# Small tables change places with a pad: the large buffers of a 28,000-instruction kernel move by 128 or 192 bytes

## The reference

```python
for l in range(DEPTH):                                   # 2 layers
    mix = token_mixer(h, w_in[l], ...)                   # h @ w_in (1024 x 9232), two attention branches,
                                                         # w_pa, w_pb and w_o (each 1024 x 1024)
    h = layer_norm(ALPHA * h + mix, ln1_g[l], ln1_b[l])
    if l % 2 == 0:
        f = swiglu(h, ...)                               # layer 0: dense, hidden width 2816
    else:
        f = moe_swiglu(h, ...)                           # layer 1: 8 experts, 2 chosen per token, hidden 3584
    h = layer_norm(ALPHA * h + f, ln2_g[l], ln2_b[l])
return h[:, N_META:]

def swiglu(x, w_gate, w_up, w_down):
    return (jax.nn.silu(x @ w_gate) * (x @ w_up)) @ w_down
```

## The kernel before

| buffer | before | mod 256 | after | mod 256 |
|---|---|---|---|---|
| raw | 4224 | 128 | 4352 | 0 |
| w_hi, w_lo | 53376, 77952 | 128 | 53504, 78080 | 0 |
| hF, acc | 102528, 111232 | 128 | 102656, 111360 | 0 |
| hT_hi, hT_lo | 115776, 126016 | 64 | 115904, 126144 | 192 |
| tab (the identity first) | 136256 | 64 | 136384 | 192 |
| mT, zT, o_tok, sgA, sgB (row 0) | from 147680 | 224 | from 147488 | 32 |
| aT_hi, aT_lo | 147776, 175936 | 64 | 147584, 175744 | 128 |
| x, S, ST, xg, a_sl, ag, y (experts) | from 147776 | 64 | from 147584 | 128 |

## Time and profile before

### The profile page before, as it was taken

How to read it: one execution, slowest core, us unless ns; L and a number is a source line. 1 busy time by engine, 2 the same in 40 slices (tenths; PEclk the granted TensorE clock), 3 DMA queues, 4 the chain that set the end, 5 groups by cost and what they waited for, 6 DMA issues and landing times.

```text
span 1867.5 us, 28534 instructions
## 1 busy us (share of the span) xinstructions
PE 1831.5 (98%) x11042; PEld 1624.1 (87%) x11042; DVE 1389.9 (74%) x1167; ACT 1101.1 (59%) x857; POOL 37.2 (2%) x78
## 2 busy tenths in 40 slices
PE   8999999999999999999999999999999999999996
PEld 8999999999989999998888888888888888888885
DVE  4756566645556566667888888888898888888987
ACT  5544254543445442546777777777777777777774
POOL 0200100000002001000000000000000000000000
PEclk9999999999999999998999999999999999999999
DMA  8625434444535355254999999999999999899993
GB/s 326 205 97 199 159 114 180 158 159 164 197 126 198 125 199 205 94 201 164 360 371 354 364 341 351 362 369 357 358 333 363 369 357 367 333 354 362 360 370 129
DMA packets 72977, 492.76 MB, mean 264 GB/s; under 512 B 9136, under 2 KB 9904, under 8 KB 15024
## 3 DMA queue, kind: packets, MB, share of 16 engines
q1 hardware_dynamic: 68720, 482.44, 69.1%
q0 software_dynamic: 2560, 5.64, 1.1%
q10 hardware_dynamic: 1600, 3.31, 0.6%
HBM read 483.66 MB, written 1.05 MB: 260 GB/s over the span
## 4 chain that ended last, share of the span: by engine, by line
PE 58%; DVE 1%; issue 1%; ACT 0%; DVEq 0%; ACTq 0%
PE ps L719 12%; PE ps L721 12%; PE ps L720 12%; PE ps L1031 6%; PE ps L1033 5%; PE ps L1034 5%; PE ps L1014 1%; PE ps L1052 1%; PE ps L1073 0%; PE ps L1074 0%; PE ps L965 0%; PE ps L974 0%; PE ps L862 0%; PE ps L877 0%; PE ps L873 0%
## 5 line engine op out<-in xcount | busy, mean ns | idle before, releaser
L1760 DVE TENSOR_TENSOR w_lo<-raw,w_hi 128x2048 fp32r<-128x2048 f32 x336 | 763.1, 2289 | 124.6 <-ACT w_hi L1179 122.3
L1179 ACT ACTIVATE w_hi<-raw 128x2048 fp32r<-128x2048 f32 x336 | 637.8, 1918 | 180.3 <-PE ps L1034 97.2
L719 PE MATMUL ps<-hT_hi,w_lo 128*128 128x272 f32 (+1 forms) x1392 | 401.7, 289 | 13.1 <-DVE w_lo L429 8.8
L429 DVE TENSOR_TENSOR w_lo<-raw,w_hi 128x2048 fp32r<-128x2048 f32 (+2 forms) x130 | 277.6, 2143 | 183.7 <-ACT w_hi L422 182.7
L720 PE MATMUL ps<-hT_lo,w_hi 128*128 128x272 f32 (+1 forms) x1392 | 399.2, 287 | 0.0
L721 PE MATMUL ps<-hT_hi,w_hi 128*128 128x272 f32 (+1 forms) x1392 | 399.1, 287 | 0.0
L719 PE MATMUL ps<-w_hi,xg_lo 128*128 128x512 f32 x896 | 358.0, 400 | 1.7 <-DVE xg_lo L2150 1.7
L721 PE MATMUL ps<-w_hi,xg_hi 128*128 128x512 f32 x896 | 351.5, 392 | 0.0
L720 PE MATMUL ps<-w_lo,xg_hi 128*128 128x512 f32 x896 | 350.3, 391 | 0.0
L422 ACT ACTIVATE w_hi<-raw 128x2048 fp32r<-128x2048 f32 (+2 forms) x132 | 234.5, 1782 | 185.0 <-PE ps L721 139.2
L719 PEld LDWEIGHTS ps<-hT_hi,w_lo 128*128 128x128 f32 x1392 | 264.7, 190 | 15.6 <-DVE w_lo L429 9.1
(11 more groups left out here) (286 smaller groups left out, 1860.2 us busy)
## 6 DMA issues: line engine op xcount, KB each, us to landing
raw<-in_dense_units SPq DMA_DIRECT2D x116, 1024.0 KB, 4.9
raw<-in_moe_w_gate SPq DMA_DIRECT2D x112, 1024.0 KB, 7.1
raw<-in_moe_w_up SPq DMA_DIRECT2D x112, 1024.0 KB, 7.0
raw<-in_moe_w_down SPq DMA_DIRECT2D x112, 1024.0 KB, 7.2
raw<-in_dense_units SPq DMA_DIRECT2D x8, 512.0 KB, 4.1
v_tok<-turned_v POOLq DMA_DIRECT2D x48, 64.0 KB, 2.4
raw<-in_dense_units SPq DMA_DIRECT2D x8, 256.0 KB, 6.3
srT<-o_tok ACTq DMA_DIRECT2D x6, 272.0 KB, 4.3
```

Of the source, the lines that this page charges most:

```text
L429: nc.vector.tensor_tensor(w_lo[:, u % HALVES, 0:k * n], raw[:, u % RAW, 0:k * n], w_hi[:, u % HALVES, 0:k * n].bitcast(F32), ALU.subtract) ...
L719: nc.tensor.matmul(dst, l_lo, r_hi, start=start, stop=False)
L1179: return nc.scalar.activation(dst, src, ACT.Copy, **kw)
L1760: tt(w_lo[:, at % HALVES, :], raw[:, at % RAW, :], w_hi[:, at % HALVES, :].bitcast(F32), ALU.subtract).then_inc(lo_ready, 1)
```

## The change

It moves allocations, and nothing else. Two tables of the token mixer, `decay` and `pair_decay` (80 and 16 bytes, rounded to 128 together), are now allocated ahead of `raw`; so `raw`, `w_hi`, `w_lo`, `hF`, `acc`, `hT` and `tab` begin 128 bytes later. The pad `row_start` (192 bytes) gives way to `mv`, `rstd` and `idle_col`, which were behind `tab` and fill the same 192 bytes. What comes behind the small tables (`o_tok`, `mT`, `zT`, `aT` and all of the experts' buffers) begins 192 bytes earlier. Each engine has the same instructions in the same order as before, with the same waits; only the addresses in them differ. Line numbers behind the moved lines are one lower in the changed kernel.

```diff
+        decay = sb(ctx, "decay", [P, HEADS, NCHUNK])
+        pair_decay = sb(ctx, "pair_decay", [P, HEADS])
         raw = sb(ctx, "raw", [P, RAW, UNIT])
         w_hi = sb(ctx, "w_hi", [P, HALVES, UNIT], F32R)
         w_lo = sb(ctx, "w_lo", [P, HALVES, UNIT], F32R)
         hF = sb(ctx, "hF", [P, KT, T])
         acc = sb(ctx, "acc", [P, 4, T])
-        sb(ctx, "row_start", [P, 48])
+        mv = sb(ctx, "mv", [P, 3, 4, 2])
+        rstd = sb(ctx, "rstd", [P, 3, 4])
+        idle_col = sb(ctx, "idle_col", [P, 1])
         hT_hi = sb(ctx, "hT_hi", [P, KT, ROW], F32R)[:, :, 0:T]
         hT_lo = sb(ctx, "hT_lo", [P, KT, ROW], F32R)[:, :, 0:T]
...
-        idle_col = sb(ctx, "idle_col", [P, 1])
         stats = acc[:, 3, 64:136].rearrange("p (t h i) -> p t h i", t=3, h=4)
-        mv = sb(ctx, "mv", [P, 3, 4, 2])
-        rstd = sb(ctx, "rstd", [P, 3, 4])
         shift = sb(ctx, "shift", [P, 3, 4])
-        decay = sb(ctx, "decay", [P, HEADS, NCHUNK])
-        pair_decay = sb(ctx, "pair_decay", [P, HEADS])
```

## The result

The changed kernel takes 1881.64 us in the median of four runs (1879.8 to 1882.23), against 1869.93 for the kernel before in the same comparison: a ratio of 1.0062, 95% interval 1.005 to 1.0074. It is slower, and outside the forecast range.

A forecast was written before the change was run, and what follows sets the result against it. PE's own matmul pitch was taken as the bound. The terms +0.5 (`aT`), -8.9 (experts) and +1 (waits) summed to -7.4 us, from 1869.4 to 1862 us, with a range of 1851 to 1872.

The forecast's parts named there:

- What bounds the kernel: Experts' stretch, half of the time: PE's own matmul pitch binds, 228.8 ns each; feeders and DMA do not.
- The distance sets the pitch, not the place: All matmul streams: pitch follows moving minus stationary operand address modulo 256 bytes, with losses of 10 to 15.5 ns.
- no effect: Rival: place modulo 64 bytes counts, or weights come no faster than 356 GB/s; 1869 us, chance 0.27.
- Items 1 and 2, dense part: `hT`, `zT` and `mT` past weights: distances stay or only change order over the rows, 0 us.
- Item 3, aT: 528 matmuls of `aT` past weights, distance -64 to 128: +1 ns each, +0.5 us, ends 0 and +1.3 us.
- Item 4, the experts: 4032 matmuls of 512 columns, distance +64 to 128: pitch 226.6 ns against 228.8, -8.9 us.
- the bad end: Experts' matmuls at distance 128: the 2.2 ns step from distance 0 to 64 taken once more, +8.9 us.
- Item 6, the small waits: Splitting on ACT and DVE: PE's waits for `w_lo` could grow from 8.4 to 9.5 us; +1 us taken.
- slower, about 1878 us: Rival: operand streams collide worse at 128 than at 64; experts 231 ns, +8.9 us, `aT` +1.3 us; chance 0.12.
- point of decision of 230.2 ns: Experts' pitch from which the slower rival is taken to hold: 228.8 ns plus 5.6 us over 4032 matmuls.
- much faster: Rival: distance 128 is farthest from collision and loses 10.0 ns or so, like +32; about 1850 us, chance 0.13.
- Item 7, DMA: Transfer targets move from 128 to 0: any gain is hidden because SP waits for buffers, 0 us.

The follow-up runs named there:

- the two crossed runs: Changed kernel with both pads 64 bytes larger, restoring the old distances: 1870.39 us, 0.9997; kernel before with both pads cut to 32 bytes, distance 128: 1880.22 us, 1.005.
- the map: Changed kernel, experts at distance 0, `aT` at -64, plus 44 series of 24 filler matmuls over distances, places, widths: 512 columns took 227.9 ns at 0, 232.5 at 128.

## Why the prediction was wrong

- **What bounds the kernel:** right. PE's own pitch, with feeders and DMA behind it, in every run.
- **The distance sets the pitch, not the place:** right, and shown by the two crossed runs, ratios 0.9997 and 1.005, and by the map at four places. It sets it not quite alone: the same distance has shown two levels, 3.3 to 4.5 ns apart. The rival "no effect" is out.
- **Items 1 and 2, dense part:** right. `hT` keeps 123.4 and 119.9 ns as the mean of all its back-to-back starts, and `zT` 125.1 and 118.5, before and after.
- **Item 3, aT:** right in sign, too small: +3.3 ns and +1.8 us, beyond the ends of +2.5 ns and +1.3 us.
- **Item 4, the experts: this step failed, and with it the sign.** I took 13.3 ns as the loss of 512 columns at distance 128, from rows of 256 columns, on the ground that whole multiples of 256 bytes belong together. The loss measured there is 232.4 - 213.3 = 19.1 ns. Even the bad end, a loss of 17.7, was short. That its +8.9 us are near the measured +8.2 is luck: the loss at 128 was set too low and the pitch before as well, since the stream averaged 230.4 ns and not the 228.8 of one chunk. The map shows why the transfer was wrong: at 128, 256 columns lose 12 ns, about what I had worked out, and 512 lose 19; at +32 it is 10 against 20. The only 512-column matmuls that the trace had at another distance, 0, were the scatter's, 64 in all and in groups too short to read. I should have said that for 512 columns one distance was known, +64, and nothing else, and set both ends equally far from it.
- **Item 6, the small waits:** right in kind. They shrank from 8.4 to 5.3 us as PE slowed and grew to 9.6 as it sped up. At distance 0 they took back 4.5 us of 10.8, though I had +1 us for them. They are the smaller part of why the +3.5 ns x 4032 = 14 us between the two chunks became 8.2. The larger part is the reading of the kernel before: over the whole stream the pitch grew by 2.1 ns, or 8.5 us.
- **The rivals:** "slower, about 1878 us" was the case that came, with its mechanism, somewhat slower still, and beyond its point of decision of 230.2 ns. I gave it 0.12, arguing that the level would have to fall steeply on both sides of 128. It doesn't: at 512 columns +96 and -96 are worse still. The argument against "much faster" misread the rows too: at 256 columns +96 loses 13.3 ns, just as distance 0 does.
- **Item 7, DMA:** right, as far as the crossed runs show: targets at 0 instead of 128 gave the time of before.

What stays open is why the distance counts. That reading the next stationary operand collides with reading the moving one is an idea that the map neither shows nor rules out: no run took one of the two away, and the pattern of good distances by width is not explained. Nor is it known what makes a stream settle at the one or the other of two pitches.

## What to carry to other kernels

Where matmuls run back to back, measure their pitch as start to start and vary the distance of the two operands modulo 256 bytes with a pad ahead of one of them: here two pads of 32 to 256 bytes each were worth from -0.5% to +0.8% of the kernel. Alignment as such bought nothing: with the weights at a multiple of 256 bytes the kernel took 1863, 1870 or 1882 us, by where the tokens lay. Don't carry a level from one width to another: a few dozen filler matmuls per distance at the width in question give the whole row in one profile, to about 1 ns. And don't take one chunk for the stream: read the pitch over all of it.

## What was not expected of the hardware

- 256 columns at distance -64 run at 114.2 ns on average over the series, against 119.6 at 0 and 120.0 at +96: 5% between distances.
- At 512 columns a distance of 16 bytes is as good as 0 (5.44 / 24 = 226.7 ns), and one of 32 is not (233.3).
- One pair of operands can settle at 123.3 or 126.7 ns, and the experts' stream at 228.8 or 233.3. At 1.2 GHz the same pair ran at 226.7 ns, without any loss: the loss was seen at the full clock alone.
